# 24 modulation columns computed by TensorE ahead of the inverse pass, its right-hand products on four array quarters, two chains to a PSUM bank

## The reference

```python
# each block scales, shifts and gates by rows made of a vector c
mod = jax.nn.silu(c) @ ada_w[l] + ada_b[l]          # 6 * 1024 outputs; 6 * 1024 more for block two
sh_m, sc_m, g_m, sh_f, sc_f, g_f = jnp.split(mod, 6, axis=-1)
...
h = modulate(rms_norm(x, mix_norm_w[l]), sh_m, sc_m)
y_r = rwkv7_group(...)      # 8 heads of 64: a recurrence, done here in 8 chunks of 64 tokens
x = x + g_m[:, None, :] * y
```

## Time and profile before

| | us |
|---|---|
| median of 3 runs (1914.72 to 1923.91) | 1919.54 |
| the profiled execution's own time | 1917.12 |
| its span in the profile | 1915.4 |
| TensorE busy (matmuls) | 1739.8 |
| VectorE busy | 1010.1 |
| ScalarE busy | 552.7 |
| GpSimd busy | 860.7 |

### The profile page before, as it was taken

The page is one execution under the profiler, slowest core; times in us unless marked ns, Lnnn a source line. Parts: engine busy times, 40 slices in busy tenths (PEclk is TensorE's granted clock), DMA queues, the critical chain, the costliest instruction groups (busy, mean ns, idle before and its releaser), DMA issues.

```text
span 1915.4 us, 26932 instructions
## 1 busy us (share of the span) xinstructions
PE 1739.8 (91%) x10840; PEld 1272.6 (66%) x10840; DVE 1010.1 (53%) x1386; ACT 552.7 (29%) x995; POOL 860.7 (45%) x408
## 2 busy tenths in 40 slices
PE   6999878998797785999989899999999899999997
PEld 4868658875333332687767667677777678888885
DVE  6576797544111113495867958665798832222112
ACT  4341462433222223324433424564100120100000
POOL 0421236431111013044343342424888968788884
PEclk8999989999799897999999999999999999999999
DMA  8821223434699997122222222213457223233331
GB/s 304 320 88 56 66 84 121 174 147 187 263 420 419 420 417 278 60 88 78 66 74 59 66 67 59 74 56 121 152 199 258 99 77 99 89 98 98 101 99 66
DMA packets 68660, 290.51 MB, mean 152 GB/s; under 512 B 9664, under 2 KB 9664, under 8 KB 56256
## 3 DMA queue, kind: packets, MB, share of 16 engines
q1 hardware_dynamic: 61776, 271.53, 39.4%
q10 hardware_dynamic: 2160, 8.91, 1.2%
q0 software_dynamic: 4608, 8.40, 1.2%
HBM read 282.25 MB, written 14.94 MB: 155 GB/s over the span
## 4 chain that ended last, share of the span: by engine, by line
PE 51%; issue 18%; POOL 13%; DMA 8%; DVE 5%; ACT 3%; POOLq 0%; SPq 0%; DVEq 0%; ACTq 0%
PE bank L2729 50%; DMA arena<-weights_dram 8%; POOL lo_ring L2672 6%; POOL hi_ring L2700 4%; POOL lo_ring L2702 3%; PE bank L2733 1%; DVE arena L2319 1%; DMA arena<-h_dram,slot_table 0%; DVE hT L2632 0%; DVE arena L1115 0%; DVE arena L2390 0%; DVE arena L1154 0%; DVE arena L701 0%; DMA late<-mod_weights_dram 0%; ACT arena L2146 0%
## 5 line engine op out<-in xcount | busy, mean ns | idle before, releaser
L2672 POOL TENSOR_TENSOR lo_ring<-ring,hi_ring 128x1024 fp32r<-128x1024 f32 x52 | 153.5, 2955 | 233.2 <-ACT hi_ring L2666 233.2
L2729 PE MATMUL bank<-h_lo,hi_ring 128*128 128x512 f32 x648 | 257.1, 397 | 0.0
L2729 PE MATMUL bank<-arena 64*64 64x64 f32 (+4 forms) x1880 | 207.5, 363 | 42.0 <-DMA arena<-weights_dram 31.8
L2729 PE MATMUL bank<-mix_h_hi,lo_ring 128*128 128x512 f32 x576 | 230.6, 400 | 0.0
L2702 POOL TENSOR_TENSOR lo_ring<-ring,hi_ring 128x1024 fp32r<-128x1024 f32 x77 | 208.8, 2712 | 6.0
L2729 PEld LDWEIGHTS bank<-arena 64*64 64x64 f32 (+2 forms) x1880 | 107.1, 154 | 127.3 <-issue 109.9
L2729 PE MATMUL bank<-mix_h_hi,hi_ring 128*128 128x512 f32 x416 | 168.6, 405 | 19.1 <-POOL lo_ring L2672 8.6
L2700 POOL TENSOR_TENSOR hi_ring<-ring,col 128x1024 fp32r<-128x1024 f32 x77 | 159.2, 2068 | 55.7 <-PE bank L2729 55.2
L2319 DVE SCALAR_TENSOR_TENSOR arena<-bank,col,arena 128x511 f32<-128x511 f32 (+14 forms) x240 | 156.5, 723 | 0.0
L2729 PEld LDWEIGHTS bank<-h_lo,hi_ring 128*128 128x128 f32 x648 | 123.2, 190 | 27.9
L2729 PE MATMUL bank<-ffn_h_hi,lo_ring 128*128 128x512 f32 x352 | 139.2, 395 | 0.0
(11 more groups left out here) (445 smaller groups left out, 3902.0 us busy)
## 6 DMA issues: line engine op xcount, KB each, us to landing
ring<-weights_dram SPq DMA_DIRECT2D x200, 512.0 KB, 3.5
arena<-weights_dram SPq DMA_DIRECT2D x61, 1024.0 KB, 25.7
arena<-mod_weights_dram SPq DMA_DIRECT2D x54, 512.0 KB, 4.5
late<-mod_weights_dram SPq DMA_DIRECT2D x42, 512.0 KB, 3.6
ring<-weights_dram SPq DMA_DIRECT2D x15, 1024.0 KB, 28.9
hT<-weights_dram SPq DMA_DIRECT2D x10, 1024.0 KB, 28.9
late<-weights_dram SPq DMA_DIRECT2D x5, 1024.0 KB, 28.4
arena<-y_dram ACTq DMA_DIRECT2D x8, 512.0 KB, 6.9
```

What stands on the lines that cost most here:

```text
L2672: pool.tensor_tensor(ring_r[:, u % RING, :], ring[:, u % RING, :], hi_unit(u).bitcast(F32), ALU.subtract).then_inc(S("split"), 1)
L2729: return pe.matmul(out, lhsT, rhs, start=start, stop=stop, skip_group_check=True)
```

## The change

Columns 40 to 63 leave VectorE. Their weights are laid out anew on the host (contraction on the partitions) and loaded into the 6 slots of `ring`, which the last projections free. TensorE makes them in six batches of four columns: for each of the 8 contraction blocks, four matmuls with silu(c) spread over 32 columns of the array, so that the four columns of a batch stand in four 32-column groups of one bank. ScalarE copies each batch out (`rows_out`), and TensorE transposes the batches in front of `left(1, 0)` (`mod_columns`); VectorE adds the bias. The loads of c for block one's second half and its activation go.

The inverse pass keeps its matmuls and changes their place: `over_chains` issues the transposed and the plain product of both chains in turn, on the four 64x64 quarters of the array; the two chains share a bank by halves of 256 columns, and the two products have separate banks. `left` uses one bank for both chains on two quarters, `level_zero` four quarters. ScalarE's copy and VectorE's subtraction become one instruction of 512 columns for both chains, the latter in two parts.

```diff
         def pe_rwkv(pe, mm, flip, take, out_half):
+            def mod_rows(b):
+                slot, before = ROW_LANDED[b % 3]
+                out = take(("mod_rows", b), ("mod_rows_out", b + 1))
+                pe.wait_ge(*at_count("silu_col", 1))
+                pe.wait_ge(*at_count(f"mod_landed{slot}", before + 64 * (b // 3 + 1)))
+                for k in range(KD):
+                    for j in range(4):
+                        n = 4 * b + j
+                        c = (KD if MOD_LATE + n >= 48 else 0) + k
+                        last = mm(out[32 * j:32 * j + 32, 0:P], silu_col[:, c:c + 1].broadcast_to([P, 32]),
+                                  ring[:, (ROW_FIRST + n) % RING, k * P:k * P + P], k == 0, k == KD - 1)
+                last.then_inc(S("mod_rows"), 1)
...
+            mod_rows(0)
             pe.wait_ge(*at_count("r_lora", 2))
...
+            mod_rows(1)
             for n in range(RW):
                 out = take(("kk_sum", n), ("kk_floor", n + 1))
...
+            mod_rows(2)
             for n in range(RW):
                 out = take(("g_up", n), ("gate_r", n + 1))
                 mm(out[:, :], g_up[:, n * P:n * P + P], r_proj[:, G_TILE, PAD:TP]).then_inc(S("lora_done"), 1)
+            mod_rows(3)
+            mod_rows(4)
+            mod_rows(5)
...
+            def over_chains(k):
+                for w in range(2):
+                    for i in range(4):
+                        for x, q in enumerate(chains(k)):
+                            c = (w + x) % 2
+                            yield q, chunk_half(c), chunk_half(1 - c), slice(i * 64, i * 64 + 64), slice(256 + i * 64, 256 + i * 64 + 64), slice(x * 256 + i * 64, x * 256 + i * 64 + 64)
...
             def right(l, k):
-                out = [take(("xx", l, q), ("inv", n_level(l, k, x))) for x, q in enumerate(chains(k))]
-                for x in range(2):
-                    pe.wait_ge(*at_count("prod", n_prod(l, k, x)))
...
+                pe.wait_ge(*at_count("inv", n_level(l - 1, k, 1)))
                 if l < 5:
-                    for x, last in crossed(k, plain):
-                        last.then_inc(S("xox_done"), 1)
+                    turned = take(("turned", l, k), ("inv", n_level(l, k, 0)))
+                plain = take(("plain", l, k), ("inv", n_level(l, k, 1) if l < 5 else n_last(k)))
+                pe.wait_ge(*at_count("prod", n_prod(l, k)))
+                for q, own, other, a, b, to in over_chains(k):
+                    if l < 5:
+                        last_b = mm(turned[other, to], inv2[own, q, a], prod[own, q, a])
+                    last_a = mm(plain[own, to], prod[own, q, a], inv2[own, q, a])
...
+            mod_columns(0, 4)
+            mod_columns(4, 2)
             left(1, 0)
...
-                modulate(MOD_LATE + k, MOD_LATE + k + 1)
...
-                done = [MOD_LATE + 4 + min(20, x + sum(x > y for y in (9, 11, 13, 15))) for x in (s, s + 1)]
-                modulate(*done)
-            mod_bias(MOD_LATE, MOD_OUT)
...
+            def load_rows(n):
+                if n < RING:
+                    sp.wait_ge(*at_count("unit_done", in_units - RING + n + 1))
+                else:
+                    sp.wait_ge(*at_count("mod_rows", (n - RING) // 4 + 1))
+                sp.dma_start(ring[:, (ROW_FIRST + n) % RING, :], mod_w_d[MOD_LATE + n]).then_inc(S(f"mod_landed{ROW_LANDED[n // 4 % 3][0]}"), 16)
             for i in range(MOD_ARENA + 5, MOD_LATE):
                 load_mod(i)
-            sp.wait_ge(*at_count("lora_done", 3 * RW))
-            sp.dma_start(silu_c2, c_d[1:2, :].broadcast_to([P, D])).then_inc(S("c_2_landed"), 16)
-            for i in range(MOD_LATE, MOD_OUT):
-                load_mod(i)
+                for n in range(2):
+                    load_rows(2 * (i - MOD_ARENA - 5) + n)
+            for n in range(RING, MOD_OUT - MOD_LATE):
+                load_rows(n)
```

More of the change, by code:

```diff
@@ L110 @@
     "x_turned": ("moe_w4", 80),
-    "moe_w5": ("qk_done", 4),
+    "mod_turned": ("qk_done", 4),
+    "moe_w5": ("mod_turned", 2),
     "states_done": ("moe_w5", 80),
@@ L742, in n_level, with n_last, n_prod, of_chains @@
             return 8 * l + 2 * k + x + 1
-        def n_prod(l, k, x):
-            return 8 * (l - 1) + 2 * k + x + 1
+        def n_last(k):
+            return n_level(4, 3, 1) + k + 1
+        def n_prod(l, k):
+            return 4 * (l - 1) + k + 1
+        def of_chains(x, k, lo=0, hi=256):
+            first, last = chains(k)
+            return x[:, first:last + 1:last - first, lo:hi]
+        def by_chain(x):
+            return x.rearrange("p (x n) -> p x n", x=2)
         def four(x):
             return x.rearrange("p (h t) -> p h t", h=4)
+        def mod_rows_in(b):
+            return late[:, 2, b % 4 * P:b % 4 * P + P] if b < 4 else late[:, 2, 512 + b % 4 * P:512 + b % 4 * P + P]
         def pe_rwkv(pe, mm, flip, take, out_half):
+            def mod_rows(b):
[10 more added lines that the diff above has]
+                last.then_inc(S("mod_rows"), 1)
+            def mod_columns(b, count):
+                out = take(("mod_cols", b), ("mod_cols", b // 4 + 1))
+                pe.wait_ge(*at_count("mod_rows_out", b + count))
+                for i in range(count):
+                    last = flip(out[:, i * P:i * P + P], mod_rows_in(b + i))
+                last.then_inc(S("mod_turned"), 1)
+            mod_rows(0)
             pe.wait_ge(*at_count("r_lora", 2))
@@ L785, in pairs @@
                             tok = slice(tt * P + 64 * c, tt * P + 64 * c + 64)
+                            into = chunk_half(1 - c if kind == "ab" and i == 0 else c)
                             for par in range(2):
                                 rows = slice(64 * par, 64 * par + 64)
-                                last = mm(out[par][64 * c:64 * c + 64, i * 256 + j * 64:i * 256 + j * 64 + 64], lhs[rows, j, tok], rhs[rows, j, tok])
+                                last = mm(out[par][into, i * 256 + j * 64:i * 256 + j * 64 + 64], lhs[rows, j, tok], rhs[rows, j, tok])
                                 if j == 3 and i == 1 and c == 1:
@@ L804, in level_zero @@
                     pe.wait_ge(*at_count("level", n_level(0, k, x)))
[L805 to L816 removed]
+                turned = take(("turned", 0, k), ("inv", n_level(0, k, 0)))
+                plain = take(("plain", 0, k), ("inv", n_level(0, k, 1)))
+                for q, own, other, a, b, to in over_chains(k):
+                    last_b = mm(turned[other, to], level_t[other, q, a], ident[other, other])
+                    last_a = mm(plain[own, to], ident[other, other], level_t[other, q, a])
+                last_b.then_inc(S("xox_done"), 1)
+                last_a.then_inc(S("xox_done"), 1)
             def values(k):
@@ L829, in left @@
             def left(l, k):
-                for x, q in enumerate(chains(k)):
+                for x in range(2):
                     pe.wait_ge(*at_count("level", n_level(l, k, x)))
-                    pe.wait_ge(*at_count("inv", n_level(l - 1, k, x)))
-                out = [take(("ox", l, q), ("prod", n_prod(l, k, x))) for x, q in enumerate(chains(k))]
-                def one(x, q, rows, half, c, i):
-                    return mm(out[x][rows, c], level_t[rows, q, c], inv2[rows, q, 256 + i * 64:256 + i * 64 + 64])
@@ L838, in left @@
[L838 to L857 removed]
+                pe.wait_ge(*at_count("inv", n_level(l - 1, k, 0)))
@@ L1017, in act_rwkv @@
                 act.activation(gate_r[:, n, :], bank[at[("g_up", n)]][:, :], ACT.Copy).then_inc(S("gate_r"), 1)
+            for b in range(3, 6):
+                rows_out(b)
             for n in range(RW):
```

146 lines of the change are left out of this document (77 added, 69 removed).

## The result

| | before | after |
|---|---|---|
| median of 5 runs, us | 1919.54 | 1929.54 |
| profiled span, us | 1915.4 | 1927.4 |
| start of the pass | 267.71 | 289.92 |
| end of the pass | 370.43 | 383.27 |
| the pass | 102.72 | 93.35 |

What follows compares the result with a forecast made beforehand. TensorE was taken to bound the kernel, with the refill of its instruction pages setting the pass's pace. 1917.1 - 15 + 17 = 1919.1, given as 1920 us; range 1905 to 1938, the forecast's own 1911 to 1930.

Steps and rivals of the forecast that it cites:

- The pass: Inverse pass on TensorE: 24 instruction pages set its pace, 88 us against 102.7, so minus 15 us.
- the page: TensorE's instruction refill in the pass: about 250 records take 3.6 us without other loads, ends 3.4 and 4.0.
- The front: TensorE ahead of the pass: six batches and their row loads delay its start, plus 17 us, from 12 to 23.
- The batch at full clock: One batch of 32 matmuls on TensorE, on four column groups ahead of the pass: 1.9 us.
- the four cycles: Batches 2 to 5 ahead of the pass: each follows the last after 5.0 + 1.9 + 0.2 = 7.1 us.
- the row loads' share of the queue: VectorE's chain to decay_up: column 39 comes 0.7 us late because a row load shares the engines with its load.
- The rest: silu(c) as columns, six ScalarE copies ahead of the pass, SyncE's dropped modulation wait: nothing.
- Rival 1: Pass: the page stays at 4.35 us and the pass gains nothing, 1934 to 1936; chance 0.14.
- Rival 2: Pass: refill is no limit, it runs at the work's pace, some 75 us, 1906 to 1909; chance 0.08.
- Rival 3: Batches ahead of the pass: column groups do not overlap, 1940, or 1926 at 3.5 us a batch; chance 0.12.
- Rival 4: Pass: row halves take turns at a shared bank, 2.9 us a step more, about 1985; chance 0.03.
- Rival 5: Ahead of the pass: loads land in 3.8 us, clock full, 10 us late only, 1909 to 1914; chance 0.10.

Runs made afterwards that it cites:

- second profiles: Kernel before and changed kernel, each unedited and run once more: ratios to before 0.9997 and 1.0059, passes of 102.48 and 90.51 us.
- Quarters only: Kernel before with only the pass edited to four array quarters, the 24 columns still on VectorE and their loads inside the pass: 0.9994 times before.
- batches only: Changed kernel with the pass as before, crossed products on two array halves and a bank for each chain: 1933.1 us, 1.0078 times before.
- loads back: Changed kernel with 22 loads of 0.5 MB, which nothing reads, put back into the pass: 1.0109 times before.
- after again: Changed kernel run once more, unedited: 1.0059 times the kernel before.
- spread 2: Changed kernel with eight row places, batches 1 to 5 issued later on TensorE and VectorE's column 39 behind the last shift: 1909.36 us, 0.9963 times before.

## Why the prediction was half right

**The pass (predicted -15, from -5 to -20; measured -9.4, and -12.0 between the second profiles).** The mechanism was right: gaps at nearly every page, loads as the cause of most of the gain, and the quarters worth little. Quarters only, with the loads left in, saved 0.6 us; batches only saved 6.9; loads back cost 7.9; four more pages cost 15, with as much more array work. What was mis-sized is the page. I took 3.6 us from one window of 3.71 that had a gap of 0.60 in it, reasoning that the page could still be a little shorter. It measured 3.94 over 18 pages, and 3.81 in the second profile. 18 x 0.34 is 6.1 us; the pass was 5.4 longer than the 88 forecast. The window of 3.71 was no more than one page (from one instruction packet to the next it was 3.4 to 4.5 us in the changed kernel's two passes), and its gap of 0.60 was no slack that could be taken off: it was the end of the wait for the next packet.

**The front (predicted +17, from 12 to 23; measured +22.2).** The batch at full clock was right, 1.95 us against 1.9, and so was the landing for the last two batches, waits of 5.1 us against 5.0. Three terms were short. First, the four cycles took 33.1 us against 28.4. The last two batches took 3.64 and 3.43 us, and the granted clock behind the wait was 0.50 for the first of them; the cycle of a batch there was 8.7 and 8.5 us, not 7.1. I had seen the same fall behind an idle 5.8 us and gave it 2 us for everything; these two batches alone were 3.2 us over. The rest is the cycle of batch 2, 8.9 us at full clock: its rows were there 6.9 us after batch 1 had let them go, not 5.0, and why they took longer no run shows. Second, upstream: I gave 0.7 us for the row loads' share of the queue, and the program lost 2.4 there. By the traces it is the multiply of 3.44 us, whose place in the buffer the next column's load needs: that load went out 2.2 us later and the next multiply waited for it. Third, 2.1 us of that execution's start were chance. About 1 us went the other way: behind batch 5, bonus_sum and the transposes took 5.3 us, not 6.3. Against the second profiles the front is 290.55 - 269.69 = 20.9 us.

**The rest (predicted nothing).** Right: the span behind the pass was 1545.0 and 1544.1 us, and 1542.5 to 1548.9 over all profiles.

**The rivals.** Rival 1, a page that stays at 4.35, is out, though it names the number of kernels with loads. Rival 2, refill no limit, is out by quarters only, and by the changed kernel's own 18.9 us of gaps at full clock. Rival 3 is out: four column groups did overlap, 64 records in 1.95 us, which is also under the 2.2 us that the prediction named beside its own 1.9. Rival 4, taking turns at a shared bank, is out: the round of right fell to 1.16 us with two row halves writing one bank. The rule of the Trainium skill that it rested on (TensorEngine Tiling (Array Packing), Gotcha 1) has no cost here where the two halves write different partitions. The other rule of the Trainium skill, that page crossings are mostly hidden (Runtime: NRT & Kernel Launch, Instruction fetch mechanics), does not hold in this pass, where 18.9 of 93.4 us are such gaps. Rival 5, a shorter front, did not come.

**The sum.** Both terms went the same way, 5.6 us in the pass and 5.2 in front, and the forecast of 1920 became 1929.5: inside its own range of 1911 to 1930, but past the line of 0.5% where I had the smaller chance. Two parts of the sum did not follow from its terms. The 2.4 us between the profiled execution and the median would have made 1919.1 into 1921.5 and not 1920, and the ends of the terms, -8 to +18, reach 1937 and not 1930.

## What to carry to other kernels

Where an engine's gaps are called "issue" in the middle of equal work, count its instructions by pages: there a faster array buys little and less other traffic does; more instructions cost 3.7 us a page here, and fewer were not tried. Work taken out of such a stretch must go where the engine idles, and its loads must run a batch further ahead than the work; the same six batches started the pass 21 to 22 us later in one arrangement and 0.6 us later in another (other places, two more slots, column 39 moved). Take the price of a page from many pages, not from the cleanest one.

## What the hardware showed that I had not expected

- A page, some 250 records of 64x64 matmuls and weight loads, took 3.7 to 4.0 us on average with no other traffic (3.4 to 4.5 one by one in the changed kernel), although its packet took only some 1.1 us: in after again the packet began 1.1 us or more after TensorE had gone on with the page before, and TensorE went on 1.2 us or more after it had landed. With a DMA share of 0.4 a page took 4.25 to 4.4 us.
- VectorE and GpSimd, started 0.01 us apart, ran 1.22 and 3.50 us; 0.07 us apart, 3.44 and 2.42. In the first case GpSimd took 1.1 us longer, in the second VectorE 2.2. The Trainium skill (SBUF — State Buffer, section "SBUF: two separate sides") has the rule that their shared pair of ports is locked for a whole instruction; the traces agree in that one of the two always runs at its own pace and the other is longer by about the time of the first. They add that which one it is can turn on less than 0.1 us, and move a chain by 2 us through the buffer that the slower one frees. The recorded starts do not tell who gets the ports: GpSimd's record starts first in both cases. That this order is what cost the 2.4 us was read from the traces and not tried by itself; in spread 2, where column 39 was moved, decay_up began 29.1 us after a multiply of 3.44 us.
- Four groups of 32 columns run side by side: 32 matmuls of the program, 64 records of 128 columns, in 1.95 us, 61 ns a matmul.
